# Two of four output pairs of the last group by seven block products

## The chip, the cores and the metric

The kernel runs on one core of one Trainium2 chip. A core has five engines that work side by side, each through its own queue in order: TensorE (PE in the profile; its weight loads are PEld), VectorE (DVE), ScalarE (ACT), GpSimd (POOL) and SyncE (SP, which here only issues DMA transfers). They wait for each other through semaphores. The metric is the device time of one execution in microseconds (us), the median of the timed runs.

## The reference

Two blocks stand one behind the other. The first mixes gated linear attention, a second recurrence and cross attention; the second is a convolution module and an MLP. The change touches only the MLP's second product and what hangs on it:

```
def sq_relu_mlp(h, w1, w2):
    return jnp.square(jax.nn.relu(h @ w1)) @ w2
...
xl = xl + g2_l * sq_relu_mlp(modulate(rms_norm_2(xl, norm2_g[i]), sh2_l, s2_l),
                             mlp_w1[i], mlp_w2[i])
...
return rms_norm_2(xl, final_g)
```

There are 1024 tokens and 1024 features, and 4096 hidden features. `w2` is 4096 x 1024. All is float32.

## The kernel before

**Exact float32 products.** Each operand is split into a high part (rounded for the fast matmul format) and a low part (the rest). A product of 128x128 weights with 128x512 data is three matmuls: high by high, high weights by low data, low weights by high data. The high part is a copy on ACT (`WH` of weights, `OPH` of data, `SUMH` of weight sums), the low part a subtraction (`WL`, `OPL`, `SUML`) on POOL, or on DVE for the weights of units that go by seven products.

**The second product.** Its 32 tiles of hidden features are taken in 8 groups (`HG`) of 4 (`GT`). A group has four units, one for each pair of output tiles (`j2` = 0 to 3); unit (g, j2) is 4 x 2 tiles of `w2` in one buffer of four. Plain, a unit is 2 output tiles x 2 token halves x 4 tiles x 3 = 48 matmuls of 512 columns. In the first seven groups (`LAST` is 7) each unit is done by Strassen's scheme instead: seven products of blocks (`TERMS`), each of 2 x 3 = 6 matmuls, so 42. `part(g, j2, m)` is block product m of such a unit, and `part_out` (DVE) adds it to the residual `RES`. Product m = 2 stays in its bank over groups.

**What the seven products need beside.** Sums of weight quarters (S1 to S4): four DVE instructions (`w_sum`) per unit, made ahead during the MLP's first product. For 28 units they are made in falling order n = 27 ... 0 in three buffers by turns: `s_load(n)` fetches the weights (`SUMW`), `w_sum(n)` writes `SUMR`, `s_store(n)` puts the sums into DRAM. `s_load(n)` waits until the sums of n+3 are made; units 2, 1, 0 stay in their buffers. Later `sum_load` brings the others back, `sum_split` makes `SUMH` and `SUML`. Sums of data blocks: `op_sum` on DVE (`OPT`), for m = 5, 6, 4, 7; T2 (m = 6) is made from T1 (m = 5), T4 (m = 4) from T2. `operand(q, m)` makes `OPH` and `OPL` of block m of pair q (q = 2g, 2g+1), in one of 24 slots; a slot is free when the block that was in it has been used in unit (g, 3) of its group. The low part of m = 6 is made in place of T2, so POOL waits there until T4 exists.

**Order.** A planner (`make_plan`) writes one list of pieces; each engine's program is this list with only its own kinds. So the order on every queue is fixed. During the first product (`hidden(i, h)`: 24 matmuls into one bank, then on ACT `RL` and `HR`, and a store of `HR`) `sums_step` takes three halves of a step of the sums each time; before `hidden(30, 1)` whatever is left of the sums is put in at once (`if i == 4 * HG - 2: for _ in sums: pass`). Then units 201, 202, 203 of the weight plan are loaded and split: the first three of the second product. The six banks of the hidden products go by turns; `hidden(30, 1)` has bank 0, as have `part(0, 0, 1)` and `part(0, 0, 6)` behind it.

In the second product the parts of two units are interleaved: (n,1), (n-1,7), (n,2), (n,5), (n,6), (n-1,4), (n,3). The operands of the next group are made beside (`operands_ahead`).

**The last group.** Group 7 is plain (`out_pair`, `out_halves`, matmuls on line 1954): pair 0 for both token halves, then pairs 1, 2, 3 for the first half, then the same for the second. Its data operands are 8 (four blocks of two pairs). Between the second half's products the norm of the first half is made (`last_norm`: `n4_sum`, `n4_row`, `final`). After the last product comes the norm of the second half: squares, column sums (PE line 2048), a root (POOL), a row (PE line 2063), eight multiplications (`final` on DVE) and their stores.

## Time and profile before

| | us |
|---|---|
| median of 3 timed runs | 2000.97 (2000.82 to 2003.54) |
| the profiled execution's own time | 1998.49 |
| its span, first to last instruction | 1996.7 |
| PE busy | 1964.0 |
| DVE, POOL, ACT busy | 1254.3, 927.4, 852.9 |
| DMA | 284.34 MB, mean 142 GB/s |

The span is what the trace shows; 1.8 us of the execution lie around it. PE is busy for 98% of it, and matmuls follow each other every 0.227 us where nothing stops them (265.24 us for 1170 in the second product). The granted clock is near full speed. The other engines are free for much of the time, but each works its queue in order, so that one instruction that waits holds all behind it. The times are from the span's start.

### The profile page before, as it was taken

Reading aid. Unit: us, or ns where it says so; the run is one execution under the profiler, and the core shown is the slowest. Engines: PE = TensorE matmul, PEld = TensorE weight load, DVE = VectorE, ACT = ScalarE, POOL = GpSimd, SP = SyncE. Lnnn points to the kernel's source line nnn. Section 1 sums busy time; section 2 is a strip of 40 time slices with the busy share of each in tenths; the row PEclk is TensorE's granted clock in tenths of the full one; section 3 lists DMA queues with packets and bytes.
Section 4 is the critical chain, followed back from the end, with each engine's and each line's share of the span. In section 5 each row is a group of like instructions: output and inputs, shape, how many; then the busy total and the mean of one; then the engine's idle time right before and its main releaser. Section 6 shows DMA issues by size and latency. Waiting matters only on the chain.

```text
span 1996.7 us, 26700 instructions
## 1 busy us (share of the span) xinstructions
PE 1964.0 (98%) x10042; PEld 1649.4 (83%) x10042; DVE 1254.3 (63%) x2095; ACT 852.9 (43%) x1431; POOL 927.4 (46%) x584
## 2 busy tenths in 40 slices
PE   9999999999999999999999999999999999999997
PEld 7988988988988888888888777777788888888886
DVE  6264455446546365555579988896561845778856
ACT  5524232343543632121455557575643534333321
POOL 4521211112121334344428886686443855877851
PEclk9999999999999999999999999999999999999999
DMA  4301101011011596766335443334457886453432
GB/s 182 106 31 53 43 33 53 33 54 38 27 64 39 178 331 228 255 238 240 127 134 193 180 139 111 119 128 142 143 169 282 307 295 206 137 185 135 142 114 85
DMA packets 94047, 284.34 MB, mean 142 GB/s; under 512 B 10576, under 2 KB 10960, under 8 KB 93792
## 3 DMA queue, kind: packets, MB, share of 16 engines
q1 hardware_dynamic: 70736, 240.17, 35.0%
q10 hardware_dynamic: 23184, 42.48, 5.9%
q8 instruction: 80, 1.31, 0.3%
q14 instruction: 47, 0.39, 0.1%
HBM read 223.36 MB, written 59.24 MB: 142 GB/s over the span
## 4 chain that ended last, share of the span: by engine, by line
PE 59%; DVE 3%; ACT 3%; issue 2%; POOL 1%; DMA 0%; POOLq 0%; DVEq 0%; SPq 0%; ACTq 0%
PE B L1775 33%; PE B L2005 13%; PE B L1954 10%; PE B L2080 1%; DVE HB L2546 1%; POOL WL L3118 1%; PE B L2016 0%; ACT HB L2205 0%; DVE B L2546 0%; POOL CO L3177 0%; DMA SUMW<-wall 0%; DVE RES L2546 0%; DVE TM L2546 0%; ACT CO L2490 0%; PE B L1939 0%
## 5 line engine op out<-in xcount | busy, mean ns | idle before, releaser
L1775 PE MATMUL B<-HB,WH 128*128 128x512 f32 x2976 | 949.5, 401 | 6.3 <-ACT HB L2205 3.6
L1775 PEld LDWEIGHTS B<-HB,WH 128*128 128x128 f32 x2976 | 548.0, 189 | 129.2 <-issue 18.7
L1775 PE MATMUL B<-HB,WL 128*128 128x512 f32 x1488 | 578.0, 391 | 1.8 <-POOL WL L3118 1.8
L3118 POOL TENSOR_TENSOR WL<-RAW,WH 128x1024 fp32r<-128x1024 f32 x132 | 320.2, 2430 | 351.0 <-ACT WH L2205 349.3
L2205 ACT ACTIVATE WH<-RAW 128x1024 fp32r<-128x1024 f32 (+1 forms) x201 | 204.7, 1024 | 316.1 <-DMA RAW<-wall 298.4
L1775 PEld LDWEIGHTS B<-HB,WL 128*128 128x128 f32 x1488 | 279.6, 188 | 62.8 <-POOL WL L3118 3.1
L3116 POOL TENSOR_TENSOR WL<-RAW,WH 128x512 fp32r<-128x512 f32 x82 | 113.8, 1412 | 315.7 <-ACT WH L2205 315.6
L2546 DVE SCALAR_TENSOR_TENSOR B<-UP,vec,B 128x512 f32<-128x512 f32 x308 | 206.3, 747 | 0.0
L2546 DVE SCALAR_TENSOR_TENSOR RES<-B,modv,RES 128x512 f32<-128x512 f32 x204 | 148.0, 743 | 81.8 <-PE B L2005 59.1
L1838 PE MATMUL B<-WH,HB 128*128 128x256 f32 x768 | 153.2, 297 | 0.0
L3103 POOL TENSOR_TENSOR small<-small 128x4 f32<-128x4 f32 (+2 forms) x36 | 38.4, 1069 | 210.3 <-DVE small L2549 210.0
L2462 ACT ACTIVATE PR<-UP,vec 128x512 f32<-128x512 f32 x150 | 106.4, 726 | 64.1 <-POOL CO L3177 51.0
L3177 POOL TENSOR_TENSOR CO<-CO,PR 128x512 f32<-128x512 f32 x90 | 118.8, 1320 | 14.7 <-ACT PR L2462 2.1
L1838 PEld LDWEIGHTS B<-WH,HB 128*128 128x128 f32 x768 | 121.5, 191 | 3.3 <-issue 0.8
L1838 PE MATMUL B<-WL,HB 128*128 128x256 f32 x384 | 108.5, 282 | 0.0
L2543 DVE TENSOR_TENSOR SUMR<-SUMW 128x256 f32<-128x256 f32 x56 | 45.4, 818 | 85.3 <-DMA SUMW<-wall 85.3
L3133 POOL TENSOR_TENSOR OPL<-OPT,OPH 128x512 fp32r<-128x512 f32 x56 | 78.5, 1418 | 25.4 <-DVE OPT L2543 23.5
L3133 POOL TENSOR_TENSOR OPL<-HQ,OPH 128x512 fp32r<-128x512 f32 x50 | 78.0, 1569 | 23.9 <-ACT OPH L2205 23.8
L2005 PE MATMUL B<-OPH,SUMH 128*128 128x512 f32 x224 | 87.2, 389 | 0.0
L2005 PE MATMUL B<-OPH,SUML 128*128 128x512 f32 x224 | 87.2, 389 | 0.0
L2005 PE MATMUL B<-OPL,SUMH 128*128 128x512 f32 x224 | 87.1, 389 | 0.0
L3177 POOL TENSOR_TENSOR COB<-COB,PR 128x512 f32<-128x512 f32 x60 | 77.7, 1295 | 16.0 <-ACT PR L2462 10.3
(270 smaller groups left out, 3330.5 us busy)
## 6 DMA issues: line engine op xcount, KB each, us to landing
RAW<-wall SPq DMA_DIRECT2D x172, 512.0 KB, 3.7
MODRAW<-wmod ACTq DMA_DIRECT2D x96, 256.0 KB, 4.9
WH<-parts SPq DMA_DIRECT2D x32, 512.0 KB, 3.2
WL<-parts SPq DMA_DIRECT2D x32, 512.0 KB, 4.1
hscr<-HR ACTq DMA_DIRECT2D x64, 256.0 KB, 3.2
HQ<-hscr SPq DMA_DIRECT2D x32, 512.0 KB, 6.4
SUMW<-wall SPq DMA_DIRECT2D x28, 512.0 KB, 7.3
sums<-SUMR SPq DMA_DIRECT2D x25, 512.0 KB, 5.9
```

Of the source, the lines that this page charges most:

```text
L1775: i = pe.matmul(bank, a[:, ks], hb(part, k, h), start=k == 0 and n == 0, stop=k == 7 and n == 2)
L1838: i = pe.matmul(bank[:, tl * 256:(tl + 1) * 256], hb(part, k)[:, t * 128:(t + 1) * 128], b[:, k % 4 * 256:(k % 4 + 1) * 256], start=k == 0 ...
L1954: i = pe.matmul(bank, a[:, ks], rhs(part, h), start=k == 0 and n == 0, stop=k == 3 and n == 2)
L2005: p = pe.matmul(bank, wt[:, c:c + 128], op[:, :], start=opens and r == 0 and i == 0, stop=r == 1 and i == 2, skip_group_check=True)
L2205: return ac.activation(o, i, ACT.Copy, **kw)
L2462: ac.activation(seg(buf[:, :]), tap(f, h, k), ACT.Copy, scale=wcol(f, k)).then_inc(sig["ptap_act"], 1)
L2543: return dv.tensor_tensor(o, a, b, op)
L2546: return dv.scalar_tensor_tensor(out=o, in0=a, scalar=s, in1=b, op0=op0, op1=op1)
L3116: i = po.tensor_tensor(lo[:, c], raw[:, c], hi[:, c].bitcast(F32), ALU.subtract)
L3118: i = po.tensor_tensor(lo, raw, hi.bitcast(F32), ALU.subtract)
L3133: po.tensor_tensor(OPL[x][:, :], raw_operand(q, m), OPH[x][:, :].bitcast(F32), ALU.subtract).then_inc(sig["op_lo"], 1)
L3177: po.tensor_tensor(co, co, product_of[n][0][:, :], ALU.add).then_inc(sig["ptap"], 1)
```

## The change

`NSUM` = 30 units go by seven products: the 28 of before, and pairs 0 and 1 of group 7. The interleaved loop runs over 30 units, so the last plain products are those of pairs 2 and 3 alone, first token half, then second. Group 7 needs 16 operands instead of 8: those of the seven products, and block B12 (twice) for the plain pairs, which take their other blocks from the operands of m = 1, 2, 3. New waits of the planner (`left`) put an operand behind the product that uses its slot's former content. Two more units of sums are made ahead, stored and loaded back. The squares of the final norm are taken where the last product of an output tile is added.

```
+ALSO = 2
+NSUM = 4 * LAST + ALSO
...
-    return unit[0] == "w2" and unit[1] < LAST
+    return unit[0] == "w2" and 4 * unit[1] + unit[2] < NSUM
...
-    if g < LAST:
-        return [(2 * g + r, m) for m in (1, 5, 2, 6, 4, 3, 7) for r in range(2)]
-    return [(2 * g + r, b) for r in range(2) for b in ("B11", "B12", "B21", "B22")]
+    return [(2 * g + r, m) for m in (1, 5, 2, 6, 4, 3, 7) + (("B12",) if g == LAST else ()) for r in range(2)]
...
-        for n in range(4 * LAST - 1, -1, -1):
-            if n + 3 < 4 * LAST:
+        for n in range(NSUM - 1, -1, -1):
+            if n + 3 < NSUM:
                 piece("s_store", n + 3)
             piece("s_load", n)
...
+    def left(of):
+
+        if BEFORE[of] is None:
+            return True
+        q, m = BEFORE[of]
+        return P.nth.get(("part", q // 2, 3, m, unit_at(q // 2)), 10 ** 6) < P.kinds["part"]
...
-            if g < LAST and n in SUM_AT:
-                piece("op_sum", 2 * g + SUM_AT[n][0], SUM_AT[n][1])
+            if n in SUM_AT:
+                of = (2 * g + SUM_AT[n][0], SUM_AT[n][1])
+                while not left(of):
+                    yield
+                piece("op_sum", *of)
+            while not left((q, m)):
+                yield
             piece("operand", q, m)
...
+        if g == LAST and (again or m == 4):
+            add_sq(4, f, h)
...
-    N = 4 * LAST
+    N = NSUM
...
-    out_pair("w2", "w2_out", LAST, 0, (4,), last_part)
-    out_halves("w2", "w2_out", LAST, (4,), lambda: bg.append(last_norm(0)))
+    out_halves("w2", "w2_out", LAST, (4,), lambda: bg.append(last_norm(0)), range(ALSO, 4), last_part)
```

How the queues differ in three places follows. **SP, end of the sums**, first before. `SUMW` from `wall` is `s_load`, `sums` from `SUMR` is `s_store` (the digit of each is the unit's number modulo 3), and `RAW` of 768 columns is the weights of a unit of the second product, 201 first.

```order
L3221 DMA RAW_52<-wall 128x768
L3232 DMA sums<-SUMR0_208 128x1024
L3228 DMA SUMW0_211<-wall 128x1024
L3221 DMA RAW_52<-wall 128x768 x3
L3257 DMA HQ00_214<-hscr 128x1024
```

And with the change:

```order
L3257 DMA RAW_52<-wall 128x768
L3268 DMA sums<-SUMR2_210 128x1024
L3264 DMA SUMW2_213<-wall 128x1024
L3268 DMA sums<-SUMR1_209 128x1024
L3264 DMA SUMW1_212<-wall 128x1024
L3268 DMA sums<-SUMR0_208 128x1024
L3264 DMA SUMW0_211<-wall 128x1024
L3257 DMA RAW_52<-wall 128x768 x3
L3293 DMA HQ00_214<-hscr 128x1024
```

Between the weights of unit 201 and those of 202, 203 and 204 stand three pairs of store and load now, where one stood.

**POOL, end of its work on the second product**, before. `OPL` is the low part of an operand (from `OPT` where it is a sum, from `HQ` where not), `SUML` that of weight sums, `WL` that of plain weights; the number behind a name is its slot.

```order
L3133 TENSOR_TENSOR OPL12_254<-HQ10_216,OPH12_230 128x512
L3123 TENSOR_TENSOR SUML0_205<-SUMR0_208,SUMH0_202 128x1024
L3133 TENSOR_TENSOR OPL13_255<-HQ10_216,OPH13_231 128x512
L3133 TENSOR_TENSOR OPL22_264<-HQ11_217,OPH22_240 128x512
L3118 TENSOR_TENSOR WL_51<-RAW_52,WH_50 128x1024
L3133 TENSOR_TENSOR OPL23_265<-HQ11_217,OPH23_241 128x512
L3118 TENSOR_TENSOR WL_51<-RAW_52,WH_50 128x1024 x3
```

And with the change:

```order
L3169 TENSOR_TENSOR OPL22_264<-OPT22_288,OPH22_240 128x512
L3169 TENSOR_TENSOR OPL23_265<-OPT23_289,OPH23_241 128x512
L3169 TENSOR_TENSOR OPL16_258<-OPT16_282,OPH16_234 128x512
L3169 TENSOR_TENSOR OPL17_259<-OPT17_283,OPH17_235 128x512
L3169 TENSOR_TENSOR OPL18_260<-HQ01_215,OPH18_236 128x512
L3159 TENSOR_TENSOR SUML2_207<-SUMR2_210,SUMH2_204 128x1024
L3169 TENSOR_TENSOR OPL19_261<-HQ11_217,OPH19_237 128x512
L3169 TENSOR_TENSOR OPL20_262<-OPT20_286,OPH20_238 128x512
L3154 TENSOR_TENSOR WL_51<-RAW_52,WH_50 128x1024
L3169 TENSOR_TENSOR OPL21_263<-OPT21_287,OPH21_239 128x512
L3169 TENSOR_TENSOR OPL0_242<-HQ00_214,OPH0_218 128x512
L3169 TENSOR_TENSOR OPL1_243<-HQ10_216,OPH1_219 128x512
```

Slots 22 and 23 hold m = 6, 16 and 17 m = 4, 18 and 19 m = 3, 20 and 21 m = 7, 0 and 1 block B12. The last eight operands follow each other with one `SUML` and one `WL` between them.

**DVE, end of the program**, before. `RES` from `vec` is a `final`, `RES` from `modv` the output of a product, `small` the column sums read.

```order
L2546 SCALAR_TENSOR_TENSOR RES_59<-B4,modv_58,RES_59 128x512
L2543 TENSOR_TENSOR FIN2_292<-FIN2_292,SQ42_300 128x512
L2546 SCALAR_TENSOR_TENSOR RES_59<-B5,modv_58,RES_59 128x512
L2546 SCALAR_TENSOR_TENSOR RES_59<-RES_59,vec_56,B7 128x512 x3
L2549 TENSOR_SCALAR small_57<-B6 128x4
```

And with the change:

```order
L2582 SCALAR_TENSOR_TENSOR RES_59<-B2,modv_58,RES_59 128x512
L2582 SCALAR_TENSOR_TENSOR RES_59<-RES_59,vec_56,B7 128x512
L2579 TENSOR_TENSOR FIN2_292<-FIN2_292,SQ42_300 128x512
L2582 SCALAR_TENSOR_TENSOR RES_59<-B3,modv_58,RES_59 128x512
L2582 SCALAR_TENSOR_TENSOR RES_59<-RES_59,vec_56,B7 128x512 x4
L2585 TENSOR_SCALAR small_57<-B6 128x4
```

Four `final` stand between the last output and the reading of its sums, where three stood.

## Rows read from the trace of the kernel before

**Rows 1.** Page, part 1: busy us, share of the span, instructions.

```profile
PE 1964.0 (98%) x10042; PEld 1649.4 (83%) x10042; DVE 1254.3 (63%) x2095; ACT 852.9 (43%) x1431; POOL 927.4 (46%) x584
```

**Rows 2.** Chain that ended last, in order of time: start, us, what.

```profile
1669.30 265.24 PE B L2005 x1170
...
1941.34 25.84 PE B L1954 x114
```

**Rows 3.** Timeline of SP's queue, end of the sums: start, us, transfer.

```profile
1653.38 0.43 SPq L3232 DMA_DIRECT2D sums<-SUMR  x1
1653.86 0.43 SPq L3228 DMA_DIRECT2D SUMW<-wall  x1
1658.45 11.21 SPq L3221 DMA_DIRECT2D RAW<-wall  x3
```

**Rows 4.** Timeline of DVE, same stretch.

```profile
1659.11 0.96 DVE L2543 TENSOR_TENSOR WL<-RAW,WH 128x768 fp32r<-128x768 f32 x1 [6.68 <-ACT WH L2205]
1659.99 0.42 DVE L2543 TENSOR_TENSOR SUMR<-SUMW 128x256 f32<-128x256 f32 x1
...
1669.29 3.00 DVE L2543 TENSOR_TENSOR WL<-RAW,WH 128x768 fp32r<-128x768 f32 x1 [4.57 <-ACT WH L2205]
1672.21 0.74 DVE L2546 SCALAR_TENSOR_TENSOR RES<-B,modv,RES 128x512 f32<-128x512 f32 x1
```

**Rows 5.** Timeline of ACT, same stretch.

```profile
1662.88 0.85 ACT L2205 ACTIVATE WH<-RAW 128x768 fp32r<-128x768 f32 x1 [2.65 <-DMA RAW<-wall]
...
1665.56 2.96 ACT L2205 ACTIVATE SUMH<-SUMR 128x1024 fp32r<-128x1024 f32 x3 [0.40 <-ACT HR L2510]
```

**Rows 6.** Timeline of POOL, same stretch.

```profile
1666.70 7.84 POOL L3123 TENSOR_TENSOR SUML<-SUMR,SUMH 128x1024 fp32r<-128x1024 f32 x3 [9.67 <-ACT SUMH L2205]
```

**Rows 7.** Timeline of PE: first block product of the MLP, and its fourth.

```profile
1669.14 0.39 PE L2005 MATMUL B<-OPH,WH 128*128 128x512 f32 x1
...
1673.23 0.39 PE L2005 MATMUL B<-OPH,SUMH 128*128 128x512 f32 x1
```

**Rows 8.** Stretches: us, busy by engine, then PE clock, DMA share, GB/s.

```profile
1660.00:1661.00 1.00, 1.00 (x7) 0.81 (x6) 0.93 (x4) 0.23 (x1) 0.00 (x0) 1.00 0.96 348
...
1663.00:1664.00 1.00, 1.00 (x6) 0.82 (x5) 0.49 (x2) 0.83 (x2) 0.00 (x0) 1.00 0.00 0
```

**Rows 9.** Tile SUMW, 1600 to 1690: from issue to landing.

```profile
DMA to landing us min/median/max: 6.4/7.3/8.8
```

**Rows 10.** Tile RAW, 1600 to 1690: from issue to landing.

```profile
DMA to landing us min/median/max: 2.8/4.8/6.2
```

**Rows 11.** Chain that ended last, near the MLP's start.

```profile
1471.54 4.45 PE B L1775 x12
```

**Rows 12.** Stretches with idle PE: columns as in group 8.

```profile
1197.00:1199.00 2.00, 0.83 (x2) 0.00 (x0) 1.95 (x3) 1.96 (x3) 1.25 (x1) 1.00 0.71 244
...
1985.00:1990.00 5.00, 1.67 (x2) 0.30 (x2) 3.99 (x8) 0.00 (x0) 1.01 (x1) 0.73 0.74 276
```

**Rows 13.** Timeline of DVE, last units of group 6: outputs of two parts.

```profile
1929.14 0.75 DVE L2546 SCALAR_TENSOR_TENSOR RES<-B,modv,RES 128x512 f32<-128x512 f32 x1 [0.61 <-PE B L2005]
...
1934.58 0.75 DVE L2546 SCALAR_TENSOR_TENSOR RES<-B,modv,RES 128x512 f32<-128x512 f32 x1 [0.61 <-PE B L2005]
```

**Rows 14.** POOL by line, 1700 to 1895: busy us, mean ns, idle before.

```profile
L3133 POOL TENSOR_TENSOR OPL<-OPT,OPH 128x512 fp32r<-128x512 f32 x41 | 56.9, 1405 | 17.6 <-DVE OPT L2543 17.6
L3123 POOL TENSOR_TENSOR SUML<-SUMR,SUMH 128x1024 fp32r<-128x1024 f32 x21 | 54.4, 2595 | 2.8 <-ACT SUMH L2205 2.8
L3133 POOL TENSOR_TENSOR OPL<-HQ,OPH 128x512 fp32r<-128x512 f32 x31 | 50.0, 1620 | 16.5 <-ACT OPH L2205 16.4
```

**Rows 15.** Timeline of POOL, last group.

```profile
1922.99 1.28 POOL L3133 TENSOR_TENSOR OPL<-HQ,OPH 128x512 fp32r<-128x512 f32 x1
1927.11 2.39 POOL L3118 TENSOR_TENSOR WL<-RAW,WH 128x1024 fp32r<-128x1024 f32 x1 [2.85 <-ACT WH L2205]
```

**Rows 16.** Timeline of DVE, end of the program.

```profile
1982.88 2.05 DVE L2546 SCALAR_TENSOR_TENSOR RES<-RES,vec,B 128x512 f32<-128x512 f32 x3
1984.85 0.15 DVE L2549 TENSOR_SCALAR small<-B 128x4 f32<-128x4 f32 x1
...
1988.67 5.36 DVE L2546 SCALAR_TENSOR_TENSOR RES<-RES,vec,B 128x512 f32<-128x512 f32 x8 [0.54 <-PE B L2063]
```

More of the change, by code:

```diff
@@ L743, in out_done, with out_halves @@
                 add_sq(which, f, h)
-    def out_halves(what, out, g, last, between):
-        js = [u_get(what, g, j2, *((2,) if what == "w2" else ())) for j2 in (1, 2, 3)]
+    def out_halves(what, out, g, last, between, pairs=(1, 2, 3), at_first=None):
+        js = [u_get(what, g, j2, *((2,) if what == "w2" else ())) for j2 in pairs]
         for h in range(2):
-            for j, j2 in zip(js, (1, 2, 3)):
+            for j, j2 in zip(js, pairs):
                 for f in (2 * j2, 2 * j2 + 1):
@@ L752, in out_halves @@
                     gemm(what, j, (name,), 4, g, f)
+                    if at_first is not None:
+                        at_first()
+                        at_first = None
                     out_done(out, g, f, h, last)
@@ L1191, in operands_ahead @@
         for n, (q, m) in enumerate(todo):
-            if g < LAST and n == 10:
+            if n == 10:
                 while not late_slots[0]:
                     yield
-            if g < LAST and n in SUM_AT:
-                piece("op_sum", 2 * g + SUM_AT[n][0], SUM_AT[n][1])
+            if n in SUM_AT:
[5 more added lines that the diff above has]
+                yield
             piece("operand", q, m)
@@ L1222, in make_plan @@
     window[0] = 0
-    unit_of, writer = {}, P.writer
+    unit_of, writer, written = {}, P.writer, set()
+    sq["last"] = {}
     def part(n, m):
@@ L1241, in part_out @@
         g, j2 = n // 4, n % 4
-        if m == 2 and g < LAST - 1:
+        if m == 2 and g < last_group(j2):
             return
@@ L1245, in part_out @@
         P.before_part[g, j2, m] = writer.get((f, h))
+        again = (f, h) in written
+        if g == LAST:
+            add_late()
+            written.add((f, h))
         writer[f, h] = ("part2", j2) if m == 2 else ("part", g, j2, m)
         piece("part_out", g, j2, m)
+        if g == LAST and (again or m == 4):
+            add_sq(4, f, h)
     first = UNITS.index(("w2", 0, 0, 2))
     def unit_ahead(n, place):
-        if place == 2 and 2 < n + 1 < 4 * LAST:
+        if place == 2 and 2 < n + 1 < NSUM:
             sum_split(n + 1)
@@ L1270, in make_plan @@
         if n % 4 == 0:
-            for _ in ahead_of:
+            for _ in ahead_of if n // 4 < LAST else ():
                 pass
-            ahead_of = operands_ahead(n // 4 + 1)
+            left_over = ahead_of
+            ahead_of = operands_ahead(n // 4 + 1) if n // 4 < LAST else iter(())
         order = [(n, 1), (n - 1, 7), (n, 2), (n, 5), (n, 6), (n - 1, 4), (n, 3)]
@@ L1282, in make_plan @@
             at_ = 7 * (n % 4) + place
-            late_slots[0] = at_ >= 26
+            late_slots[0] = at_ >= 26 or n // 4 == LAST
+            if n // 4 == LAST:
+                next(left_over, None)
             if at_ >= 3 and (at_ % 4 != 2 or at_ == 26):
@@ L1326, in last_norm @@
             piece("final", h, k)
-    sq["last"] = {}
-    out_pair("w2", "w2_out", LAST, 0, (4,), last_part)
-    out_halves("w2", "w2_out", LAST, (4,), lambda: bg.append(last_norm(0)))
+    out_halves("w2", "w2_out", LAST, (4,), lambda: bg.append(last_norm(0)), range(ALSO, 4), last_part)
     drain()
@@ L1597, in build_program @@
         for p in P.order:
-            if p[0] == "part" and p[3] == 2 and p[1] < LAST - 1:
+            if p[0] == "part" and p[3] == 2 and p[1] < last_group(p[2]):
                 part2_n[p[1:3]] = len(part2_n) + 1
@@ L1641, in wait_part @@
         def wait_part(w, g, j2, m):
-            if m == 2 and g < LAST - 1:
+            if m == 2 and g < last_group(j2):
                 w.wait_ge(sig["part2"], part2_n[g, j2])
@@ L1670, in wait_mlp_read, with wait_written @@
             wait_full(w, "part", LAST - 1, 3, 4)
+        def wait_written(w, f, h):
+            wait_taken(w, *(P.writer[f, h] if f < 2 * ALSO else ("w2_out", LAST, f, h)))
         def mix_buf(e):
@@ L2006, in part @@
                                       stop=r == 1 and i == 2, skip_group_check=True)
-                if m == 2 and g < LAST - 1:
+                if m == 2 and g < last_group(j2):
                     p.then_inc(sig["part2"], 1)
@@ L3414 @@
     hscr = nc.dram_tensor("hscr", (4 * HG, 128, T), F32, kind="Internal").ap()
-    sums = nc.dram_tensor("sums", (4 * LAST, 128, 1024), F32, kind="Internal").ap()
+    sums = nc.dram_tensor("sums", (NSUM, 128, 1024), F32, kind="Internal").ap()
     build_program(nc, *aps, out, oscr, parts, hscr, sums)
```

22 lines of the change are left out of this document (13 added, 9 removed).

## Prediction

> **What bounds the kernel now.** I read the page's busy times first: PE has work in 98% of the span and no other engine in more than 63% [rows 1]. Then the chain of waits, in order of time: from the start of the MLP's second product to the norm it is PE alone, 265.24 us for 1170 matmuls in the block products and 25.84 us for 114 in the plain ones, 0.2267 us each in both [rows 2]. So a matmul less is worth 0.2267 us, and a stop of PE costs its full length, since nothing behind it has slack to give back. Third, the timelines of each queue at the three places where the orders differ: the end of the sums, the operands of group 7, and the norm at the end. What matters there is how late each supplier may be. At the first place it is almost nothing. `part(0,0,6)` needs bank 0, which DVE frees with the output of `part(0,0,1)`, 1672.21 plus 0.74 = 1672.95 [rows 4]; PE begins it at 1673.23 [rows 7]. That is 0.28 us to spare.
>
> **What goes.** Two units at 48 matmuls become two at 42: 12 x 0.2267 = 2.7 us less of PE. That is 0.14%, smaller than the 0.2% (4.0 us) that a measurement of this kernel can tell from no change. So the outcome hangs on the suppliers.
>
> **The sums' end.** Two units more go through a process with a fixed pace, and the leftover is put in before `hidden(30,1)`. Up to the load of unit 201 the transfers go out at the old times. From there, on the old clock:
> 1. SP issued one store and one load at 1653.38 and 1653.86, and the weights of 202 at 1658.45 [rows 3]. Now the second pair (store 4, load 1) can go at once, since the sums of 4 are made; the third pair (store 3, load 0) needs the sums of 3.
> 2. The sums of 3 take the place on DVE that those of 1 had: behind the split of unit 201, from 1659.99 in four instructions of 0.42 us [rows 4], done at 1661.6. So load 0 goes at 1662.1, and only then, on SP in order, the weights of 202, at 1662.6 instead of 1658.45.
> 3. When they land: the DMA engines move 348 GB/s up to 1662 and nothing in 1663 to 1664 [rows 8], so the old work ended at about 1662.2. Without the 0.39 MB of unit 202 that is 1661.1. The second pair adds 1.05 MB or 3.0 us (1664.1), the third 3.0 us (1667.1), unit 202 1.1 us (1668.2). With the 0.7 us that lay between the last bytes and ACT's start at 1662.88 [rows 5] ACT gets it at 1668.9: 6.0 us late.
> 4. On ACT the high part of 202 stands ahead of the relu of `hidden(30,1)` (which frees bank 0 for the first block product), that ahead of the three `SUMH` (at 1665.56 before), and these ahead of the split of 203. All move by 6.0 us. The sums of 0 are ready sooner (load 0 at 1667.8, plus 1.6).
> 5. POOL's first `SUML` then ends not at about 1669.1 but 1675.1, and `part(0,0,5)` wants it at 1672.3. DVE's split of 203, 1669.29 for 3.00 us, and the output behind it move by 6.0 too, so bank 0 is free at 1678.95 instead of 1672.95. Against 1673.23 PE has lost 5.7 us by then, in three stops. Later units need nothing that moved more than PE has.
>
> Bounds. If the queue held nothing up, the weights of 202 would land 2.8 us after their issue, the fastest of this stretch [rows 10], at 1665.4: 2.5 us late, a loss of 2.2. If load 0 takes the stretch's median of 7.3 [rows 9], 1669.4, and unit 202 comes 1.1 behind it, with the same 0.7, that is 1671.2: 8.3 late, a loss of 8.0. I take 5.7, the sum of bytes, in the middle and nearest to the pace of the rows.
>
> The trace shows landings of 6.4 to 8.8 us for these loads, each right behind a store [rows 9]: they queue. The Trainium skill ("DMA: Bandwidth & Descriptors", "Queues, rings and completion order") says that each DMA engine takes the descriptors of a ring in order; by that the weights of 202 cannot overtake the pairs before them, and without it the loss would be 2.2 instead of 5.7.
>
> DVE's split of 768 columns took 0.96 us with POOL idle and 3.00 beside POOL's `SUML` [rows 4, 6]. The Trainium skill ("SBUF — State Buffer", "Who interferes with whom") says that a VectorE instruction with two SBUF inputs and a GpSimd instruction that reads SBUF shut each other out for a whole instruction; POOL runs the same three `SUML` in the same relation, so by that the 3.00 stays, and if it fell to 0.96 the loss would be 3.7.
>
> **The clock.** In these 5.7 us of stops, PE would do some 4.1 us of work in 9.8. In the trace, 2 us with 0.83 busy stayed at full clock, and 5 us with 1.67 busy had a mean granted clock of 0.73, so part at 1.2 GHz [rows 12]. Once at the lower level, 12 matmuls took 4.45 us [rows 11] instead of 2.72: 1.7 us. Before `part(0,0,6)` only 1.4 us of work lie in about 6.5 us, nearer to the second row. I take one fall: 1.7 (bounds 0 and 3.5 for two, the second at the next place).
>
> **Operands of group 7.** POOL must make ten operands where T4 of the group waits for slot 16, free when `part(6,3,5)` has run; its output starts on DVE at 1929.14 [rows 13]. Then DVE does this output (0.75), the split of unit 230 (0.96) and T4 (0.7): 1931.5. Only then can POOL start `OPL22`. At the means of 1.405 for sums, 1.62 for blocks and 2.595 for `SUML` [rows 14], and 2.39 for `WL` [rows 15]: four sums (5.6, plus 0.2 for the second T4), `OPL18` 1.6, `SUML` 2.6: 1941.5; `OPL19` 1943.1; `OPL20` 1944.5; `WL` 1946.9; `OPL21` 1948.3. PE, where the output of `part(6,3,7)` was at 1934.58 [rows 13], now has one part ahead of it, so each part of 1.36 us puts the start of (7,0,3) at 1941.2 and of (7,0,7) at 1943.9; their second low operand is wanted 0.9 later. (7,0,3) waits 1.0 for `OPL19`, and (7,0,7) then wants `OPL21` at 1945.8 and gets it at 1948.3, 2.5 later: 3.5. With 1.28 for each `OPL` [rows 15] and 2.4 for `SUML` the end is 1946.8 and the loss 2.0. By nearness to unhindered POOL in a stretch where DVE has little else, I take 2.8; bounds 0 (T4 earlier than I read) and 3.7. The steady groups have no such stop, because there T4 finds its slot free long before.
>
> **The end.** Four `final` instead of three stand ahead of the reading of the sums. Three took 2.05 and the reading followed at 1984.85, right at their end [rows 16], so a fourth delays the root, the row and the eight finals behind it: 0.7. Bounds 0 and 0.75. From `n4_sum` to `n4_row` of the first half PE still has 15 matmuls to do, as before, so no stop is added there.
>
> **At nothing.** Seven outputs a unit instead of four on DVE, 8 more high parts on ACT, two loads of sums: these engines idle in the last group, and the transfers are issued a unit ahead. If that cover fails it is the stop of a part, under 1 us. The transfers of two more sums (4.2 MB) count above only where they collide.
>
> **Sum.** -2.7 + 5.7 + 1.7 + 2.8 + 0.7 = +8.2 us. On the profiled execution 1998.49 + 8.2 = 2006.7; the median of the runs lies 2.5 above that execution, so 2000.97 + 8.2 = 2009.2.
>
> **Rivals.**
> A. Both stops, but the clock holds, as in the row of 1197: +6.5, 2007.5. For: no single stop is over 3 us. Against: the share of work is far lower than in that row. 0.27.
> B. Only one of the two stops is there. If POOL keeps up, -2.7 + 5.7 + 1.7 + 0.7 = +5.4, 2006.4; if the sums' end costs the least and POOL 2.8, -2.7 + 2.2 + 2.8 + 0.7 = +3.0, 2004.0. Against the first: twelve POOL instructions in a row after a start that DVE fixes. 0.15.
> C. Not slower: the queue of transfers is empty when load 0 and the weights of 202 go out, as it was in 1663 to 1664 [rows 8], and they arrive within the fastest times. Place: ACT's wait for unit 202. Price 2.2, POOL 2.0, no fall of the clock: -2.7 + 2.2 + 2.0 + 0.7 = +2.2, 2003.2, within the bound. It decides when unit 202 lands before 1667.2, 4.3 us late. 0.11.
> D. The change does what its matmul count says, with no stop: -2.7 + 0.7 = -2.0, 1999.0, and with the end at 0 and the runs' scatter it could pass -4.0. For it speaks that POOL and DMA are idle on the whole; against it that 0.28 us are to spare where 6 come. 0.05.
> My forecast (two stops, one fall) has 0.42.
>
> **Range and chances.** The forecast's bounds and A reach from 2005 to 2013, B and C down to 2003. Held 8 in 10: 2003.5 to 2012.5. Faster by over 0.2% 0.03; within it (1997.0 to 2005.0) 0.17; slower 0.80.
>
> **What the profile after would show.** 10030 matmuls. PE waits on bank 0 or ACT's relu at the start of `part(0,0,1)`, on `SUML` in `part(0,0,5)`, on DVE's output at `part(0,0,6)`, 5.7 us in all around 1669 to 1679, with the weights of unit 202 issued near 1662.6. A granted clock under 1 right behind. In group 7 a wait on POOL's `OPL` at (7,0,3) and (7,0,7). The reading of `small` 0.7 us later behind the last output. I am wrong if PE runs through 1669 to 1680 without idle time, or if `OPL21` ends before 1945 on the old clock plus the first stop.

## The result, and the profile after

| | before | with the change |
|---|---|---|
| median of the timed runs, us | 2002.51 (1998.23 to 2006.03, 8 runs) | 2013.86 (2008.34 to 2018.03, 8 runs) |
| the profiled execution's own time | 1998.49 | 2016.09 |
| its span | 1996.7 | 2014.2 |
| mean granted clock of PE | 0.996 | 0.991 |
| matmuls | 10042 | 10030 |

The ratio is 1.0056, 95% interval 1.0043 to 1.0068. The change makes the kernel slower by 11.4 us in this series; forecast were +8.2 us and at most 2012.5. A second series of the same kernel gave 1.0048 (1.0031 to 1.0065), +9.6 us. So the sign and the places of the loss came as forecast, and the size was too small.

Below, a stop is idle time of PE between two matmuls, and a fall is a time in which its granted clock is at the lower level.

The two spans differ by 17.5 us, more than the medians. Of that, 6.4 us arise ahead of the MLP and are scatter of the execution: in a second profile of the same changed kernel the long run of hidden matmuls starts at 1476.59, where the kernel before has 1476.85. To leave them out I measure from the start of the long run of hidden matmuls of the second half, which stands in the chain of waits (start, us, what). Before:

```profile
1476.85 192.45 PE B L1775 x849
```

With the change, the chain from there to the end of the second product:

```profile
1483.29 176.18 PE B L1811 x777
1659.49 5.02 DMA RAW<-wall
1669.08 5.96 DMA RAW<-wall
1678.46 1.99 ACT SUMH L2241 x2
1681.21 2.95 DVE WL L2579
1684.87 258.56 PE B L2041 x1128
1947.81 5.97 POOL OPL L3169 x4
...
1958.59 2.39 POOL WL L3154
1962.25 10.52 PE B L2041 x38
```

Where PE stood alone [rows 2], the chain now leaves it twice, for the weights of 202 and for POOL's operands. From the start of the hidden run to the span's end, the stretch, it is 519.85 us before and 530.91 after: **+11.06 us**. In the second profile of the same kernel it is 530.61. Within that run nothing differs by more than 0.04 us up to the issue of unit 201's weights. That issue (1653.01 before, 1659.49 after, so 6.48 later) is the clock against which I read the next rows. PE's timeline at the sums' end (start, us, instruction, then the idle time before it and what ended it):

```profile
1676.49 0.47 PE L2041 MATMUL B<-OPH,WH 128*128 128x512 f32 x1 [0.71 <-issue]
...
1681.06 0.50 PE L2041 MATMUL B<-OPH,SUML 128*128 128x512 f32 x1 [1.11 <-POOL SUML L3159]
...
1684.87 0.80 PE L2041 MATMUL B<-OPH,SUMH 128*128 128x512 f32 x1 [2.61 <-DVE RES L2582]
```

These are the three stops that were forecast, each with its releaser. `part(0,0,6)` starts 25.38 us after the weights of 201 were issued, against 20.22 before [rows 7]: 5.16 us late. SP's queue:

```profile
1659.49 0.33 SPq L3257 DMA_DIRECT2D RAW<-wall  x1
1659.86 0.49 SPq L3268 DMA_DIRECT2D sums<-SUMR  x1
1660.39 0.43 SPq L3264 DMA_DIRECT2D SUMW<-wall  x1
1660.87 1.15 SPq L3268 DMA_DIRECT2D sums<-SUMR  x1
1662.06 0.98 SPq L3264 DMA_DIRECT2D SUMW<-wall  x1
1667.99 0.33 SPq L3268 DMA_DIRECT2D sums<-SUMR  x1
1668.36 0.68 SPq L3264 DMA_DIRECT2D SUMW<-wall  x1
1669.08 7.06 SPq L3257 DMA_DIRECT2D RAW<-wall  x3
```

Less 6.48, the weights of 202 go out at 1662.60, where 1662.6 was forecast and 1658.45 stood before [rows 3]. ACT, DVE and POOL follow:

```profile
1675.06 0.85 ACT L2241 ACTIVATE WH<-RAW 128x768 fp32r<-128x768 f32 x1 [8.53 <-DMA RAW<-wall]
...
1677.49 2.95 ACT L2241 ACTIVATE SUMH<-SUMR 128x1024 fp32r<-128x1024 f32 x3 [0.44 <-ACT HR L2546]
```

```profile
1681.21 2.95 DVE L2579 TENSOR_TENSOR WL<-RAW,WH 128x768 fp32r<-128x768 f32 x1 [4.31 <-ACT WH L2241]
1684.08 1.40 DVE L2582 SCALAR_TENSOR_TENSOR RES<-B,modv,RES 128x512 f32<-128x512 f32 x2
```

```profile
1678.63 7.75 POOL L3159 TENSOR_TENSOR SUML<-SUMR,SUMH 128x1024 fp32r<-128x1024 f32 x3 [15.00 <-ACT SUMH L2241]
```

ACT gets unit 202 at 1668.58 on the old clock; 1668.9 was forecast, 1662.88 stood before [rows 5]. DVE's split of 203 takes 2.95 us beside POOL's `SUML`, as the 3.00 before [rows 4, 6], and the output that frees bank 0 stands behind it. The windows show the clock (us, busy of each engine, then PE's granted clock, DMA share, GB/s):

```profile
1682.00:1684.00 2.00, 0.26 (x2) 0.00 (x0) 2.00 (x1) 1.59 (x3) 2.00 (x2) 0.87 1.03 416
1684.00:1686.00 2.00, 1.13 (x3) 0.94 (x4) 1.48 (x3) 0.42 (x2) 2.00 (x1) 0.50 0.69 274
...
1688.00:1690.00 2.00, 2.00 (x6) 1.60 (x5) 0.59 (x1) 0.00 (x0) 0.84 (x1) 0.50 0.00 0
1690.00:1692.00 2.00, 2.00 (x9) 1.59 (x9) 0.91 (x2) 0.00 (x0) 0.00 (x0) 0.92 0.00 0
```

0.50 is the lower of the two levels, 1.2 GHz: six matmuls fall into 2 us instead of nine. It sets in during the third stop, before PE goes on at 1684.87. The first operand sum on DVE behind it (`OPT`, 1679.57 before, 1693.89 after) is 14.32 us later, or 7.84 on the shifted clock; less the 5.16, this fall cost **2.7 us**. In group 7 POOL reads:

```profile
1945.82 1.30 POOL L3169 TENSOR_TENSOR OPL<-OPT,OPH 128x512 fp32r<-128x512 f32 x1 [6.05 <-DVE OPT L2579]
...
1960.93 1.26 POOL L3169 TENSOR_TENSOR OPL<-OPT,OPH 128x512 fp32r<-128x512 f32 x1
```

The last of the rows is `OPL21`, done at 1962.19. `OPL22` starts at 1945.82, less 14.32 exactly the forecast 1931.5. PE and the clock there:

```profile
1957.43 0.50 PE L2041 MATMUL B<-OPL,SUMH 128*128 128x512 f32 x1 [0.86 <-POOL OPL L3169]
1962.25 0.50 PE L2041 MATMUL B<-OPL,SUMH 128*128 128x512 f32 x1 [1.80 <-POOL OPL L3169]
```

```profile
1960.00:1962.00 2.00, 0.45 (x2) 0.02 (x1) 0.33 (x1) 0.00 (x0) 2.00 (x2) 1.00 0.00 0
1962.00:1964.00 2.00, 1.75 (x6) 1.43 (x7) 0.75 (x1) 0.20 (x1) 2.00 (x3) 0.84 0.00 0
1964.00:1966.00 2.00, 2.00 (x6) 1.57 (x5) 1.43 (x2) 0.51 (x2) 0.68 (x1) 0.50 0.00 0
1966.00:1968.00 2.00, 2.00 (x8) 1.60 (x8) 1.33 (x2) 1.51 (x2) 0.33 (x1) 0.80 0.00 0
```

A **second fall** of the clock stands behind the second stop: 0.16 + 0.50 + 0.20 of 2 us each, 1.7 us. Last, the end on DVE:

```profile
1998.68 0.75 DVE L2582 SCALAR_TENSOR_TENSOR RES<-B,modv,RES 128x512 f32<-128x512 f32 x1 [0.60 <-PE B L1990]
1999.35 2.71 DVE L2582 SCALAR_TENSOR_TENSOR RES<-RES,vec,B 128x512 f32<-128x512 f32 x4
2001.98 0.15 DVE L2585 TENSOR_SCALAR small<-B 128x4 f32<-128x4 f32 x1
```

Four `final` take 2.71 us where three took 2.05 [rows 16]. From the last output (1998.68) to the span's end it is 15.52 us, against 14.49 before.

| term, us | forecast | measured | how |
|---|---|---|---|
| 12 matmuls less | -2.7 | -2.7 | 10030 on the page |
| sums' end | +5.7 | +5.2 | 25.38 - 20.22; second profile 5.7 |
| clock behind it | +1.7 | +2.7 | 7.84 - 5.16; second profile 1.7 |
| POOL in group 7 | +2.8 | +3.2 | from one matmul's start to the next 1.25 and 2.19 where 0.23 is usual, and 0.2 on the two matmuls behind |
| clock behind that | 0 | +1.7 | windows |
| end | +0.7 | +1.0 | 15.52 - 14.49 |
| sum | +8.2 | +11.1 | span's end: +11.06 |

### The profile page after: what moved, and what is told of

The parts are those of the page before. It is cut to its first block, busy times and chain, and to the rows that moved or that the text cites. A ratio compares the mean times of both kernels' runs of the same rounds, so it can differ in the third digit from the quotient of the medians.

```text
span 2014.2 us, 26732 instructions
## 1 busy us (share of the span) xinstructions
PE 1971.1 (98%) x10030; PEld 1652.9 (82%) x10030; DVE 1265.7 (63%) x2117; ACT 859.1 (43%) x1441; POOL 937.4 (47%) x592
## 4 chain that ended last, share of the span: by engine, by line
PE 83%; DVE 5%; ACT 4%; issue 3%; DMA 2%; POOL 2%; ACTq 0%; SPq 0%; POOLq 0%; DVEq 0%
PE B L1811 42%; PE B L2041 13%; PE B L1990 8%; PE B L1874 7%; PE B L1912 4%; DMA RAW<-wall 2%; PE B L1939 1%; PE B L1942 1%; PE B L1936 1%; POOL WL L3154 1%; PE B L1975 1%; ACT WH L2241 1%; DVE HB L2582 1%; PE B L2116 1%; PE B L1959 1%
## 5 line engine op out<-in xcount | busy, mean ns | idle before, releaser
L3154 POOL TENSOR_TENSOR WL<-RAW,WH 128x1024 fp32r<-128x1024 f32 x130 | 315.6, 2433 | 335.4 <-ACT WH L2241 333.7
L3169 POOL TENSOR_TENSOR OPL<-OPT,OPH 128x512 fp32r<-128x512 f32 x64 | 89.2, 1411 | 42.6 <-DVE OPT L2579 40.6
L2579 DVE TENSOR_TENSOR SUMR<-SUMW 128x256 f32<-128x256 f32 x60 | 47.4, 797 | 90.3 <-DMA SUMW<-wall 90.3
L2041 PE MATMUL B<-OPH,SUMH 128*128 128x512 f32 x240 | 95.0, 396 | 2.6 <-DVE RES L2582 2.6
L2041 PE MATMUL B<-OPL,SUMH 128*128 128x512 f32 x240 | 94.9, 395 | 2.7 <-POOL OPL L3169 2.7
L2041 PE MATMUL B<-OPH,SUML 128*128 128x512 f32 x240 | 94.7, 395 | 1.1 <-POOL SUML L3159 1.1
L2241 ACT ACTIVATE OPH<-OPT 128x512 fp32r<-128x512 f32 x64 | 40.0, 627 | 120.9 <-DVE OPT L2579 120.1
```

The costliest lines, as they stand in the source:

```text
L2041: p = pe.matmul(bank, wt[:, c:c + 128], op[:, :], start=opens and r == 0 and i == 0, stop=r == 1 and i == 2, skip_group_check=True)
L2241: return ac.activation(o, i, ACT.Copy, **kw)
L3154: i = po.tensor_tensor(lo, raw, hi.bitcast(F32), ALU.subtract)
L3169: po.tensor_tensor(OPL[x][:, :], raw_operand(q, m), OPH[x][:, :].bitcast(F32), ALU.subtract).then_inc(sig["op_lo"], 1)
```

## The experiments

In the table "first stop" is the delay of `part(0,0,6)` against 20.22 us behind the issue of unit 201's weights; "stretch" is from the start of the hidden run to the span's end, less 519.85; "norm" is the time from PE's last wait in the convolution's product to the start of the hidden run.

| kernel | first stop | clock falls in the second product | stretch | norm | timed ratio (95%) |
|---|---|---|---|---|---|
| before | 0 | none | 0 | 45.24 | 1 |
| changed | 5.16 | two | +11.06 | 44.14 | 1.0056 (1.0043 to 1.0068) |
| changed, again | 5.73 | two | +10.76 | 44.22 | 1.0048 (1.0031 to 1.0065) |
| late sums alone | 4.74 | one | +6.83 | 43.22 | 1.0036 (1.0022 to 1.0049) |
| faster sums | 0 | none | +1.56 | 47.98 | 1.0027 (1.0017 to 1.0037) |
| faster sums, again | 0 | one, group 7 | +3.18 | 45.79 | 1.0023 (1.0011 to 1.0036) |
| other operand order | 5.41 | one, first | +6.36 | 45.26 | 1.0050 (1.0036 to 1.0064) |
| filled stops | 6.05 | none | +7.83 | 43.20 | 1.0043 (1.0024 to 1.0061) |
| leftover behind 202 | 7.7 | two | +13.76 | 45.13 | one run, 2012.01 us |
| third pair behind 202 | 4.79 | two | +11.00 | 44.91 | one run, 2011.09 us |
| both mended | 0 | none | -0.42 | 47.76 | 1.0006 (0.9995 to 1.0017) |
| and three `final` | 0 | none | -1.20 | 47.55 | 1.0006 (0.9995 to 1.0016) |
| the same, again | 0 | none | -1.32 | 46.25 | 1.0008 (0.9997 to 1.0018) |
| before, faster sums | 0 | none | +0.66 | 48.97 | 1.0003 (0.9992 to 1.0013) |
| split pace, mended | 0 | none | -0.92 | 45.25 | 0.9999 (0.9988 to 1.0011) |

**Late sums alone** (`g_late`). The kernel before, with its sums started four halves later, so that three pairs stand ahead of unit 202, but none of the change's transfers or products:

```
     def sums_ahead():
+        for _ in range(4):
+            yield
         for n in range(4 * LAST - 1, -1, -1):
```

> The kernel before, with the weight sums begun four steps later, so that the same leftover of three pairs of store and load as in the changed kernel stands ahead of the weights of unit 202; bytes and matmuls are those of before. Theory (the weights of unit 202 are issued late because SyncE stands behind a store that waits for sums): the first stop as in the changed kernel, part(0,0,6) begins 25.4 us after the issue of unit 201's weights instead of 20.2, the clock falls behind it for 2.6 us more, 7.8 us in all, ratio to before 1.0039. Rival (the stop comes from the bytes of two more units of sums): nothing or under 2 us, 1.000 to 1.001.

PE's timeline:

```profile
1669.91 0.47 PE L2007 MATMUL B<-OPH,WH 128*128 128x512 f32 x1 [0.31 <-issue]
...
1674.47 0.50 PE L2007 MATMUL B<-OPH,SUML 128*128 128x512 f32 x1 [1.10 <-POOL SUML L3125]
...
1678.27 0.66 PE L2007 MATMUL B<-OPH,SUMH 128*128 128x512 f32 x1 [2.61 <-DVE RES L2548]
```

The same three releasers, in a kernel with the matmuls and bytes of before. Position in SP's queue makes the first stop, not the further 4.2 MB. The stop is 4.74 us, and the fall behind it costs 1.7 (clock 0.50 from 1679 to 1681, 0.57 in the next microsecond), so the stretch is 6.8 us longer instead of the 7.8 expected; the remaining 0.4 us is at the end. The timed ratio is clear of the rival's 1.001.

**Faster sums** (`a_pace`). The changed kernel, five halves per three turns:

```
     def sums_step():
-        turns[0] += 3
-        while turns[0] >= 2:
-            turns[0] -= 2
+        turns[0] += 5
+        while turns[0] >= 3:
+            turns[0] -= 3
```

> The changed kernel with the sums taken at 5/3 steps a time instead of 3/2, so that none are left over. Theory: unit 202's weights go out in time, the first stop and its fall of the clock are gone: 7.8 us less than the changed kernel, so 3 to 4 us over before, ratio 1.0017. Rival (the transfers are at their limit there anyway): the higher pace makes weights late in the first product, PE waits there, and at most half of the 7.8 comes back.

One pair stands between the weights of 201 and 202 again (SP's queue):

```profile
1655.06 0.33 SPq L3257 DMA_DIRECT2D RAW<-wall  x1
1655.44 0.43 SPq L3268 DMA_DIRECT2D sums<-SUMR  x1
1655.91 0.43 SPq L3264 DMA_DIRECT2D SUMW<-wall  x1
1660.50 5.77 SPq L3257 DMA_DIRECT2D RAW<-wall  x2
```

`part(0,0,6)` starts 20.22 us behind the first, to the hundredth as before. Both stops of group 7 (0.85 and 1.80) are still there, but the clock held. The interval of the timed ratio ends below that of the changed kernel in the first series, so the gain is in the timed runs too; that the ratio is above the 1.0017 expected is taken up by the last experiments.

**Other operand order** (`b_order`). T4 made later, after the blocks that need nothing:

```
+    ms = (1, 5, 6, 4, 2, 3, 7, "B12") if g == LAST else (1, 5, 2, 6, 4, 3, 7)
+    return [(2 * g + r, m) for m in ms for r in range(2)]
```

> The changed kernel with the operands of group 7 in the order m = 1, 5, 6, 4, 2, 3, 7 instead of 1, 5, 2, 6, 4, 3, 7, so that T4 gets a slot that is free early. Theory: GpSimd does four operands before the point at which it began before, its last operand of m = 7 is done in time, no wait on OPL in group 7 and no second fall of the clock: 4.8 us less than the changed kernel, ratio to before 1.0033. Rival (GpSimd's amount of work sets the stop, not T4): a stop of 2 us or more stays.

PE no longer waits for POOL in group 7, and one wait of 0.43 us for a bank is left. The first stop and a fall behind it stay, but here that fall costs 1.7 us (windows) and not 2.7. So of the 11.06 - 6.36 = 4.7 us between the two stretches 1.0 is the shorter first fall, and 0.25 is lost again to a first stop of 5.41. The 3.2 of POOL and the 1.7 of the second fall are gone; in their place stand the 0.43 and some 0.5 us that I did not find. The timed runs don't show this gain: 1.0050 measured where 1.0033 was expected, its interval overlaps both series of the changed kernel, and its lower end (+7.2 us) lies above the stretch. The profiled execution is the second fastest of seven; the two fast ones (2004.05 and 2004.25 us) have a mean clock of 0.995, the five others (2008.2 to 2012.2) one of 0.991 to 0.993. Where those lose their clock no trace shows.

**Leftover behind 202** (`c_flush`). The flush of the sums one turn later:

```
-        if i == 4 * HG - 2:
+        if i == 4 * HG - 1:
             for _ in sums:
                 pass
-        if i == 4 * HG - 1:
             for n in range(3):
```

> The changed kernel with the leftover of the sums put in one product later, behind the load of unit 202. Theory (unit 202's weights carry the stop): they go out in time; what is left is that the first SUMH waits for the sums of unit 0, made some 3.6 us later than ScalarE would be ready: part(0,0,6) begins about 23.5 us after the issue of unit 201's weights (20.2 before, 25.4 in the changed kernel). Rival (the sums of unit 0 themselves set it in the changed kernel): 25 or more.

This missed. The weights of 202 went out in time, but all three pairs moved behind them, and the sums themselves came last:

```profile
1673.19 2.95 ACT L2240 ACTIVATE SUMH<-SUMR 128x1024 fp32r<-128x1024 f32 x3 [8.38 <-DVE SUMR L2578]
```

The first stop grew to 7.7 us. The experiment moved more than the one thing that it was to test.

**Third pair behind 202** (`c2_third_pair`). Only the last store and load moved:

```
         if i == 4 * HG - 2:
+            for _ in range(4):
+                next(sums, None)
+        if i == 4 * HG - 1:
             for _ in sums:
                 pass
-        if i == 4 * HG - 1:
```

> The changed kernel with only the third pair (store 3, load 0) moved behind the load of unit 202's weights. If those weights carry the stop: they go out at the old time, 5.4 us after unit 201's, ScalarE then waits only for the sums of unit 0, some 1.5 us less late, and part(0,0,6) begins about 24 us after the issue of unit 201's weights (20.2 before, 25.4 in the changed kernel). If the sums of unit 0 carry it: 25 or more.

The stop is 4.79 us instead of 5.16 or 5.73: 25.01 us behind the issue of 201's weights, the edge of what was expected if the sums of 0 carry it. ACT, `SUMH` of units 0 to 2:

```profile
1672.19 2.95 ACT L2243 ACTIVATE SUMH<-SUMR 128x1024 fp32r<-128x1024 f32 x3 [2.33 <-DVE SUMR L2581]
```

The weights of 202 went out at the old time (5.44 us behind those of 201), but ACT got them only 7.87 us later, behind the second pair: 13.31 us behind the issue of 201, against 9.87 before and 15.57 in the changed kernel. `SUMH` then waited for the sums of 0. In the two profiles of the changed kernel these were made 1.70 and 1.64 us before `SUMH` began, as my step 4 had it; here load 0 stands behind the weights of 202, and DVE began on its data 6.73 us after its issue instead of 5.74 and 5.84. So the two chains end close to each other, each delays the other in the one queue, and moving one pair gains 0.4 to 0.9 us.

**Filled stops** (`fill`). Idle matmuls of ones into a free bank ahead of the three late parts, 10, 4 and 7 of them:

```
+                fill = {(0, 0, 6): (10, ("part", 0, 2, 1)), (7, 0, 3): (4, ("w2_out", 7, 6, 0)), (7, 0, 7): (7, ("w2_out", 7, 6, 0))}
+                if (g, j2, m) in fill:
+                    count, free = fill[g, j2, m]
+                    spare, _ = start(free)
+                    for _ in range(count):
+                        pe.matmul(spare, ones[:, :].bitcast(F32R), ones[:, 0:1].to_broadcast([128, 512]).bitcast(F32R), start=True, stop=True)
```

> The changed kernel with 10 matmuls of ones into a bank that is free, ahead of part(0,0,6), 4 ahead of part(7,0,3) and 7 ahead of part(7,0,7), each group shorter than the stop it fills. Theory (the falls of the clock follow the idle time and cost 2.7 and 1.8 us beside the stops): part(0,0,6) begins 25.4 us after the issue of unit 201's weights as in the changed kernel, the last operands come as late as there, but the granted clock stays full behind both places, and from that issue to the end of the span it is 4 us less than the changed kernel's 354.7. Rival (the price of the falls is part of the wait for the suppliers): the clock stays full and the span's rest stays within 1.5 us of 354.7.

PE's timeline and the windows there:

```profile
1673.72 2.13 PE L2019 MATMUL B<-ones 128*128 128x512 f32 x9
1676.28 0.50 PE L2047 MATMUL B<-OPH,SUMH 128*128 128x512 f32 x1 [0.43 <-DVE RES L2588]
```

```profile
1676.00:1678.00 2.00, 1.73 (x8) 1.43 (x9) 0.91 (x3) 0.62 (x1) 2.00 (x2) 1.00 0.01 4
```

The suppliers are as late as ever (first stop 6.05), but the clock holds at both places, and the stretch is 3.2 us shorter than changed (4 expected). With 0.9 us more of first stop, that is the two falls together: 4.1 against 4.4 by the rows. The timed ratio (1.0043) overlaps both series of the changed kernel, so the gain is shown by the profiles alone, and the profiled execution is the fastest of its five.

**Both mended** (`ab`), faster sums and the other order:

> Both mended: sums at 5/3 steps a time, and the operands of group 7 in the order of b_order. Theory: no stop at either place; 2.7 us of matmuls less, 0.7 to 1.0 more at the end, 0.4 for a bank in the last units: 1.3 us less than before, ratio 0.9993, not to be told from 1. Rival (something else in the change costs, as a_pace's 1.0027 against the 1.0017 expected may say): 1.001 or more.

**And three `final`** (`abd`), one `yield` less in `last_norm`:

```
             for _ in range(FINALS):
                 yield
-                yield
                 finals(1)
```

> As ab, and the second of the first half's final multiplications one step earlier, so that three and not four stand ahead of the reading of the last sums. Theory: another 0.7 us less at the end; from the last output to the end of the span 14.5 us as before instead of 15.5; 2 us less than before, ratio 0.9990. Rival (the multiplication delays the output behind it by as much as it gives): as ab.

No stop of half a microsecond is left and the clock holds; the last output is 14.84 us from the end instead of 15.52. The stretches are shorter than before by 0.4 and 1.2 us (1.3 and 2 were expected). Of the 2.7 us of twelve matmuls, 1.0 goes at the end in the one and 0.35 in the other, 0.4 to 0.65 in waits for a bank, and 0.6 to 0.8 in places that I did not find. Both timed ratios lie above that, at 1.0006, and neither can be told from no change.

**Changed, again** (`after_again`) and **faster sums, again** (`a_pace_again`):

> The changed kernel as it is, profiled once more. Theory: the stop ahead of the sums' last run belongs to the order of the program, so the last product of the last unit begins 25.4 us (25.2 to 25.6) behind the issue of the weights of unit 201 again, with the clock down to half behind it for 4 to 6 us; GpSimd's operands of the last group cost 0.86 and 1.80 us again. If the second fall of the clock also belongs to the program, windows at half clock stand behind the 1.80 us stop, and the stretch from that issue to the span's end takes 354.7 us (354.3 to 355.1). Rival: the second fall comes in some executions only; then the stretch takes about 352.9 us. Ratio to the kernel before 1.0056 (1.004 to 1.007).

> The changed kernel with the faster pace of the sums, profiled once more. Theory: no stop ahead of the sums' last run, 20.2 us from the issue of the weights of unit 201 to it. If the second fall of the clock comes in some executions only, it may stand here this time, and the stretch to the span's end then takes 347.0 us in place of 345.2; if it hangs on the program, the clock holds again at 345.2 us (345.0 to 345.5). Ratio 1.002 (1.001 to 1.0035).

The first stop came out at 5.73, a little above the expected end of 25.6; the stops in group 7 are the same to a hundredth. The fall behind the first stop was shorter (1.7 us), and the second was there. In the faster kernel the second fall came this time:

```profile
1952.00:1954.00 2.00, 2.00 (x8) 1.57 (x7) 1.19 (x2) 0.63 (x1) 1.77 (x2) 0.69 0.00 0
1954.00:1956.00 2.00, 2.00 (x6) 1.51 (x6) 1.30 (x3) 0.98 (x2) 0.00 (x0) 0.50 0.00 0
```

Stretch +3.18 instead of +1.56: 1.62 us. So the same kernel with the same stops has this fall in one execution and not in another.

**Where the faster pace costs.** The versions with faster sums time above their stretch (by 1 to 4 us). In the profiles the norm ahead of the MLP differs: with the faster pace one more store and load go out there, the weights that ACT splits land later, and the squares wait behind them. The further pair on SP, then ACT, then PE, of faster sums:

```profile
1458.31 1.10 SPq L3268 DMA_DIRECT2D sums<-SUMR  x1
1459.45 0.75 SPq L3264 DMA_DIRECT2D SUMW<-wall  x1
```

```profile
1469.44 1.06 ACT L2241 ACTIVATE WH<-RAW 128x1024 fp32r<-128x1024 f32 x1 [5.23 <-DMA RAW<-wall]
1470.41 0.61 ACT L2443 ACTIVATE SQ<-RES 128x512 f32<-128x512 f32 x1
```

```profile
1471.07 1.87 PE L2084 MATMUL B<-ones,SQ 128*128 128x1 f32 x8 [1.70 <-ACT SQ L2443]
```

Before, this wait is 0.20. Three kernels test this.

**Before, faster sums** (`before_53`), the edit of `a_pace` alone:

> The kernel before with the sums at 5 halves per 3 turns and nothing else. Theory: the cost at the norm in front of the MLP belongs to the pace: TensorE waits about 1 us for ScalarE's squares there, the clock falls, 47.3 us from the last wait in the convolution's product to the hidden run against 44.3, ratio 1.0014 (1.0004 to 1.0024). Everything behind is as before, 519.9 us. Rival: the pace is free, ratio 1.0000 (0.9992 to 1.0008).

**Split pace** (`split_pace`), the old pace up to the norm, the faster behind:

> The changed kernel with the new operand order, three final multiplications ahead of the column sums, and the pace of the sums at 3 halves per 2 turns up to the norm in front of the MLP, 20 per 12 (as 5 per 3) only behind it. Theory: the faster pace costs 2.9 us at that norm (from the last wait of TensorE in the convolution's product to the start of the long run of hidden matmuls 47.3 us on average in the four profiles with 5/3 throughout, 44.3 in seven others), since one more pair of store and load goes out ahead of the weights that ScalarE splits before the squares of the norm. So here 43.2 to 45.3 us there, no wait on ScalarE's squares above 0.3, no stop ahead of the sums' last product, and from the start of the hidden run to the span's end 518.7 us (518.3 to 519.3) against 519.9 before. Ratio 0.9992 (0.998 to 1.0003). Rival: what the timed runs of the mended versions lack against their stretch is scatter of the clock anywhere; then the ratio stays at 1.0006.

This run tells nothing of that: 2158.31 us, ratio 1.0785. My edit called its new table `pace`, a name that the planner has for its own time per matmul; it so changed the order of the work on all engines up to the MLP, with one wait of PE of 62.7 us. Renamed, and beside it the kernel with the faster pace throughout:

```
-    turns = [0]
+    turns, sum_pace = [0], [18]
...
-        turns[0] += 5
-        while turns[0] >= 3:
-            turns[0] -= 3
+        turns[0] += sum_pace[0]
+        while turns[0] >= 12:
+            turns[0] -= 12
...
+    sum_pace[0] = 20
     first_hidden(1)
```

> The changed kernel with the new operand order, three final multiplications ahead of the column sums, and the pace of the sums at 3 halves per 2 turns up to the norm in front of the MLP, 20 per 12 only behind it. Theory: the norm ahead of the MLP costs as in the kernel before, 43.2 to 45.3 us from the last wait of TensorE in the convolution's product to the long run of hidden matmuls (47.3 with the faster pace throughout), with no wait on ScalarE's squares above 0.3; from the start of that run to the span's end 518.7 us (518.3 to 519.3) against 519.9 before. Ratio 0.9992 (0.998 to 1.0003), lower than that of abd_again by 0.0010. Rival: the norm's price is no steady one; then both have the same ratio, 1.0000 to 1.0006.

> The faster pace throughout, the new operand order and three final multiplications, once more. Theory: TensorE waits about 1 us for ScalarE's squares at the norm ahead of the MLP and the clock falls there, 47.5 us from the last wait in the convolution's product; 518.7 us from there to the end. Ratio 1.0004 (0.9994 to 1.0014).

The six profiles with the faster pace throughout have 45.79 to 48.97 us at the norm, mean 47.4, and a wait of 0.89 to 1.90 for the squares. The nine with the old pace there have 43.20 to 45.26, mean 44.5, `split_b` 45.25 among them, with a wait of 0.21 at most. So a wait of 0.89 us or more is in every profile with the faster pace and in none without. A fall of the clock there is not: the kernel before has one too, with its wait of 0.20 [rows 11]. In the timed runs it is at the edge of what they can tell: `split_b` 0.9999 and `abd_again` 1.0008 on the same chip lie apart by 0.0009 (0.0010 expected) with overlapping intervals, and `before_53` came out at 1.0003, within the rival's range, just outside the theory's and 0.0011 under its value. Its stretch was expected unchanged; the +0.66 lies at the end, where the last matmuls ran at the lower clock. The price of 2.9 us is that of the profiles; shown in the timed runs it is not. `split_b` has the lowest ratio of all versions of the change, and can't be told from the kernel before.

## Why the prediction was wrong

**Right, with the sizes.** The bound: PE has no slack, and suppliers decide. The count of matmuls, -2.7. The queue at the sums' end: SP's issue of unit 202 to 0.1 us, ACT's start 0.3 us early, three stops with the releasers named, 5.2 and 5.7 us for the forecast 5.7; `g_late` shows the cause alone and `a_pace` its removal. The same stop took 4.74 to 6.05 us over five profiles with the weights of 202 behind all three pairs, so a hit to a tenth is in part luck. ACT began on the weights of 202 5.98 us after their issue, behind all pairs, and not 2.8 as the fastest of the stretch [rows 10]. That agrees with the Trainium skill ("DMA: Bandwidth & Descriptors", "Queues, rings and completion order"), by which the descriptors of a ring are taken in order. DVE's split beside `SUML` took 2.95, not 0.96; by that the rule of the Trainium skill in "SBUF — State Buffer", "Who interferes with whom", also held. POOL in group 7 started as forecast, and its two stops came where they were named; 3.2 us for the 2.8 that I had taken between 2.0 and 3.5; 0.2 of it is that the matmuls behind each stop follow a little slower. `b_order` shows in its profile that the place of T4 in the order makes these stops.

**Wrong.** The step that failed is "The clock. I take one fall: 1.7". Two falls came in both profiles of the kernel, 2.7 and 1.7 us in the first and 1.7 and 1.7 in the second. The sum has nothing for the second; it stands only in the bound ("3.5 for two, the second at the next place"), and the prediction gives no reason for leaving it out, though it had stops of 1.0 and 2.5 us by my own sum. So the term was mis-sized: 1.7 us forecast, 4.4 and 3.4 measured. `fill` shows that the falls are a price of their own, about 4 us, apart from the stops. Over the forecast the stretch has 2.9 us in the first profile and 2.6 in the second; 2.7 and 1.7 of them are this step. Why the first fall cost 2.7 us in one execution and 1.7 in another is open.

**Too small.** The end was 1.0 us instead of 0.7: the additional `final` cost 0.66, and the row for the norm ran at the lower clock, 2.05 us for the 1.67 of before. That 0.4 is not the change's: `g_late`, with three `final`, has the 2.05 too, and of the later profiles none was as short as the 1.67.

**The range.** My own terms held what came: with the first stop at 5.7, two falls at 3.5, POOL at 3.7 and the end at 0.75 they give -2.7 + 5.7 + 3.5 + 3.7 + 0.75 = +10.95, or 2011.9, within the top of 2012.5. The measured +11.35 is near that, but it stands on a median of the kernel before that moved by 1.5 us between 3 and 8 runs (2000.97, 2002.51), and for this the range had no room: on the old median the changed kernel would be at 2012.3. So the measured 2013.86 is 4.7 us over the forecast, 3.2 by the terms and 1.5 by the base. The chances (slower 0.80) were sound.

**The rivals.** A (the clock holds) is ruled out by the windows, B and C by both stops being seen at nearly full size. D is what `ab`, `abd` (twice) and `split_b` come to in their profiles, once the stops are taken away: -0.4 to -1.3 us of stretch, too little to be timed.

**What stays open.** Why the timed runs of `b_order` stand above its stretch; whether its operand order wins anything in them; and how often the second fall comes (in 2 of 2 profiles of the changed kernel, 2 of 2 of the kernels that only moved pairs, 1 of 2 of the faster one). The eight timed runs of the changed kernel have spans from 2006.4 us at a mean clock of 0.994 to 2016.1 at 0.988, and the four longest have a clock of 0.988 to 0.991, the four shortest one of 0.992 to 0.995. 0.006 of the clock over 2010 us is, as an estimate, 12 us, so falls that come or stay away could make most of that spread; only one of the eight has a trace, so this is not shown.

## What to carry over

When PE is busy for 98% and a change takes 0.14% of its work away, look first at which transfer, issued in order, stands behind the one that you add; a supplier with 0.28 us to spare turns a queue position into a stop. Price each stop of TensorE twice, by its length and by a fall of the clock behind it, and let the range hold a fall at each place with such stops: behind 0.86 and 1.80 us one came in five of six profiles. Compare a profile's gain with the timed runs before calling it one, since the profiled execution can be among the fastest. When a process with a fixed pace gets more work, look at both ends of it: slower it is late at its end, and faster it delays what stands beside its start, as the norm here.
